# A two-block transformer on one core: high and low weight matmuls in turn in eight of the stages

## The reference

```python
# first block
z = rms_norm(x) @ w_in                       # q, k, v, u, g
h = x + mixed @ w_out                        # mixed: attention and gated MLP
f = rms_norm(h)
h = h + (silu(f @ ffn_w1) * (f @ ffn_w3)) @ ffn_w2      # 2048 -> 5632 -> 2048
h = h + (p @ pl_w_up) * sigmoid(h @ pl_w_gate)
# second block, with 16 tokens put in front
proj = rms_norm(h) @ w_in_2                  # pool, conv and gate inputs
y_b = (gb_in * causal_depthwise_conv(gc_in * v_in, conv_w)) @ conv_out_w
h = h + (g_a * y_a + g_b * y_b) @ w_o
h = h + (silu(gate) * up) @ w_down           # gate, up = rms_norm(h) @ w_gate_up
out = rms_norm(h)
```

## Time and profile before

| | |
|---|---|
| median of 3 runs | 2713.7 us |
| profiled execution, whole | 2712.95 us |
| its span, first to last instruction | 2711.1 us |
| mean granted TensorE clock | 0.996 |
| TensorE busy with matmuls | 2683.8 us, 99% |
| VectorE busy | 1674.7 us, 62% |
| ScalarE busy | 1269.5 us, 47% |
| read from memory | 499.41 MB, 185 GB/s |

### The profile page before, as it was taken

How to read it: one execution, slowest core, us unless ns; L and a number is a source line. 1 busy time by engine, 2 the same in 40 slices (tenths; PEclk the granted TensorE clock), 3 DMA queues, 4 the chain that set the end, 5 groups by cost and what they waited for, 6 DMA issues and landing times.

```text
span 2711.1 us, 40123 instructions
## 1 busy us (share of the span) xinstructions
PE 2683.8 (99%) x15739; PEld 2380.8 (88%) x15739; DVE 1674.7 (62%) x1605; ACT 1269.5 (47%) x1354; POOL 0.8 (0%) x7
## 2 busy tenths in 40 slices
PE   9998999999999999999999999999999999999998
PEld 8888888888888888888999999888888888888887
DVE  6567766555655566696576656556765655565555
ACT  5455554444444444566443333444554434443445
POOL 0000000000000000000000000000000000000000
PEclk9998999999999999999999999999999999999999
DMA  8553555555555555555546555555555555555553
GB/s 294 188 171 115 178 190 189 190 190 189 186 186 187 188 190 188 179 186 187 185 158 202 178 180 187 186 186 186 188 198 189 186 192 192 190 186 191 181 186 140
DMA packets 253935, 504.02 MB, mean 186 GB/s; under 512 B 8082, under 2 KB 11076, under 8 KB 253668
## 3 DMA queue, kind: packets, MB, share of 16 engines
q1 hardware_dynamic: 251860, 497.60, 55.3%
q10 hardware_dynamic: 1952, 4.73, 0.5%
HBM read 499.41 MB, written 2.88 MB: 185 GB/s over the span
## 4 chain that ended last, share of the span: by engine, by line
PE 95%; DVE 3%; ACT 1%; issue 1%; DMA 0%; SPq 0%; DVEq 0%; ACTq 0%
PE ps L1260 47%; PE ps L1266 24%; PE ps L1279 4%; PE ps L1280 4%; PE ps L1281 4%; PE ps L1298 3%; PE ps L1297 3%; PE ps L1299 3%; DVE lo L777 1%; DMA xtok<-in_x_dram 0%; PE ps L1289 0%; PE ps L1291 0%; PE ps L1290 0%; ACT hi L472 0%; DVE work L785 0%
## 5 line engine op out<-in xcount | busy, mean ns | idle before, releaser
L777 DVE TENSOR_TENSOR lo<-raw,hi 128x1024 fp32r<-128x1024 f32 x940 | 1136.9, 1223 | 821.7 <-ACT hi L472 819.1
L472 ACT ACTIVATE hi<-raw 128x1024 fp32r<-128x1024 f32 x940 | 984.9, 1056 | 999.3 <-PE ps L1266 695.8
L1260 PE MATMUL ps<-A,hi 128*128 128x512 f32 x3648 | 914.0, 392 | 1.5 <-DVE work L785 1.5
L1260 PEld LDWEIGHTS ps<-A,hi 128*128 128x128 f32 x3648 | 656.4, 189 | 119.3 <-DVE work L785 1.7
L1266 PEld LDWEIGHTS ps<-A,lo 128*128 128x128 f32 x3648 | 497.6, 190 | 35.7 <-DVE lo L777 0.2
L1266 PE MATMUL ps<-A,lo 128*128 128x256 f32 x3648 | 508.7, 282 | 0.0
L1260 PE MATMUL ps<-B,hi 128*128 128x512 f32 x1984 | 499.6, 393 | 0.3 <-ACT hi L472 0.3
L1260 PEld LDWEIGHTS ps<-B,hi 128*128 128x128 f32 x1984 | 356.1, 188 | 66.1 <-ACT hi L472 0.5
L1266 PEld LDWEIGHTS ps<-B,lo 128*128 128x128 f32 x1984 | 269.8, 189 | 20.6
L1266 PE MATMUL ps<-B,lo 128*128 128x256 f32 x1984 | 275.6, 281 | 0.0
L1297 PE MATMUL ps<-B,hi 128*128 128x258 f32 (+1 forms) x768 | 218.5, 285 | 1.1 <-issue 1.1
(11 more groups left out here) (228 smaller groups left out, 1348.7 us busy)
## 6 DMA issues: line engine op xcount, KB each, us to landing
raw<-in_w_in_dram SPq DMA_DIRECT2D x136, 1024.0 KB, 5.1
raw<-in_ffn_w_dram SPq DMA_DIRECT2D x132, 1024.0 KB, 5.1
raw<-in_w_gate_up_dram SPq DMA_DIRECT2D x88, 1024.0 KB, 5.0
raw<-in_w_down_dram SPq DMA_DIRECT2D x44, 1024.0 KB, 5.0
raw<-in_w_out_dram SPq DMA_DIRECT2D x16, 1024.0 KB, 5.2
raw<-in_pl_w_gate_dram SPq DMA_DIRECT2D x16, 1024.0 KB, 5.1
raw<-in_conv_out_w_dram SPq DMA_DIRECT2D x16, 1024.0 KB, 5.0
raw<-in_w_o_dram SPq DMA_DIRECT2D x16, 1024.0 KB, 5.1
```

Source lines behind the costliest of these rows:

```text
L472: act.activation(hi[:, slot % RING], raw[:, raw_slot, 2 * (slot % 2):2 * (slot % 2) + 2, :], ACT.Copy).then_inc(hi_ready, 1)
L777: dve.tensor_tensor(lo[:, slot % RING], raw[:, slot // 2 % RAWS, 2 * (slot % 2):2 * (slot % 2) + 2, :], hi[:, slot % RING], ALU.subtract). ...
L1260: pe.matmul(to, high(slot, kk, m), both, start=j == 0 and kk == 0, stop=False)
```

## The change

Eight stages are named in a set: the six of the first FFN, `cout` and `wo`. In these a piece no longer runs eight high matmuls and then eight low ones. It waits for `lo_ready` at its start (and no longer for `hi_ready`), and for each block and bank runs the high matmul and right behind it the low one. The other `halves` stages (`qk`, `out`, `plup`, `plgate`, `pool`, the three up-projections of the second FFN), `wide_halves` and the rest keep their order.

```diff
+IN_TURN = {"f1_up0", "f1_down0", "f1_up1", "f1_down1", "f1_up2", "f1_down2", "cout", "wo"}
...
-                if layout in ("halves", "wide_halves") or (layout == "conv" and seg.kinds[g] == "cb"):
+                if seg.name not in IN_TURN and (layout in ("halves", "wide_halves") or (layout == "conv" and seg.kinds[g] == "cb")):
                     pe.wait_ge(hi_ready, n + 1)
...
                     for m in range(MT):
                         Wh, Wl = high(slot, kk, m), low(slot, kk, m)
-                        if layout == "packed":
+                        if layout == "halves":
+                            pe.matmul(ps[:, b0 + m, :], Wh, X[:, k, 0:2 * T], start=first, stop=False)
+                            last = pe.matmul(ps[:, b0 + m, 0:T], Wl, X[:, k, 0:T], start=False, stop=final)
+                        elif layout == "packed":
```

## The result

| | before | changed |
|---|---|---|
| median of the runs | 2713.4 us (2712.0 to 2714.5, 15 runs) | 2719.4 us (2717.4 to 2721.3, 15 runs) |
| span of the profiled execution | 2711.1 us | 2718.0 us |

The ratio is 1.0022, 95% interval 1.0015 to 1.003: slower by 0.22%, where 0.2% faster was forecast. The time lies inside the range, on the other side of no change.

A forecast was written before the change was run, and what follows sets the result against it. The prediction took TensorE's matmul start distances as the bound: 2624 pairs, each 2.2 ns cheaper, save 5.8 us, taking the span from 2711.1 to 2705.3 us and the median to 2708 us. Its 8-in-10 range was 2689 to 2729 us.

The forecast's parts named there:

- What bounds the kernel, and how many pairs change: TensorE, busy 99% of the span, sets the time by distances between matmul starts; 2624 high-low pairs change, 916 us.
- The moved wait: Waiting for lo_ready at a piece's start costs nothing: VectorE's low-part subtraction has at least 1.75 us in hand.
- The start distance read as duration less 162 ns: On TensorE, a matmul's distance to the next start is its shown duration less 162 ns, good to some 2 ns.
- The sum: In the changed stages a pair costs 347 ns (231 high, 116 low), 2.2 ns less than now: 5.8 us saved.
- my upper bound: Highest price of a pair in turn from the rows, 234 + 120 = 354 ns: 13 us lost.
- What a switch between the kinds does: On TensorE, a high soon after lows is up to 7 ns later, a low behind a high some 4 ns sooner.
- The 20 ns that I could not place: Loss per piece with one round of switches in the old order: 2794 ns against 2774 at 226.8 and 120.
- the third, in its mild form: High behind a low 234 ns, low 120 with late weight load: 354 ns a pair, 2726 us; whole rival's chance 0.23.
- its strong form: Each of eight switch rounds a piece pays 20 ns: 46 us more, 2760 us; chance 0.23 for both forms together.
- The first (340 to 343 ns): A single low doesn't disturb the highs, settled rates hold: 16 to 24 us saved, 2690 to 2697 us; chance 0.18.
- The signs: New profile: highs about 393 ns, lows about 278, unchanged second FFN; under 344 or over 350 ns a pair refutes the forecast.
- The rule weighed: Skill page's TensorE gaps, 216 and 109 ns: with a load under each matmul, 325 ns a pair in both orders.

## Why the prediction was wrong

- **What bounds the kernel, and how many pairs change**: right. Only TensorE's start distances moved, on 2624 pairs.
- **The moved wait**: right. It costs nothing in the eight stages, and the run with all stages in turn shows what it costs where the 1.75 us of the earlier trace rows are missing.
- **The start distance read as duration less 162 ns**: right for means (399 + 281 less 353.3 leaves 163 each), but not within 2 ns for one matmul. The trace of before, from start to start, has 233 ns for the first high at 905.20 where I took 234, and 113 for the first low at 907.04 where I took 116.
- **The sum** is the step that failed: "I take the middle of 340 and 354, 347 ns". Its bounds held, and 346.7 is what the fast stages measured. But it made one price for all pairs out of local readings taken in another order, and there are two prices. That 346.7 agrees with the forecast's 347 is in part luck: I took a middle between two bounds, while the fast rhythm is the sum of the settled rates, 226.8 + 120 = 346.8, which stood in the prediction only as the 2774 ns of a piece. In 2112 of 2624 pairs the price is 353.3, 0.7 ns below my upper bound; mis-sized by 6.3 ns there, 13.3 us.
- **What a switch between the kinds does** gave the wrong model, in which a matmul's distance depends on the one before it. The 20 ns that I could not place can be placed by the start distances of before, from 905.20: the eight highs take 233, 236, 228, 233, 231, 226, 227, 227 ns, 27 more than eight settled ones, and the lows 113, 119 and then 120 each, 8 less than eight settled ones. So five highs pass until the rate is settled. In turn it never gets there: in the slow rhythm highs take 233, 236 and 241, the last more than any high of that piece, and three pairs cost 1060 ns where the settled rates give 1040, the same 20 once more. How late a high is depends on several matmuls before it.
- **The rivals**: the third, in its mild form (354 ns, 2726 us), is what the first FFN did as a number; its strong form, 7 more rounds at 20 ns, did not happen. The first (340 to 343 ns) happened nowhere: in turn no high takes less than 230 ns. The convolution's output and the last projection did what the forecast said, 346.7. That different stages could go different ways was among none of them.
- **The signs**: they worked. Highs at 399 ns and 353.3 ns a pair in the first FFN said that the forecast was wrong, and that it was the slower rival; the second FFN kept its times.
- **The rule weighed**, the gaps of the Trainium skill, TensorE: Matmul & The Clock Gate, section "Back-to-back issue gap" (which gives them for a matmul apart from its weight load), would have made the order indifferent. The runs disagree, with 2773 to 2827 ns for a piece of the same matmuls.
- **The range** held the time, because it took the upper bound in.

What stays open is what in TensorE holds the rhythm, and by what rule a start or a break selects one. The runs show that the extra time of a piece fits steps of about 6.7 ns, that the rhythm goes with the stream's own past, and that a break or a stall can change it. They don't show which unit it is, and none of the models here would have told in advance which stages go fast.

## What to carry to other kernels

Where TensorE never waits and a profile still shows it above its settled rates, print the distances from start to start of single matmuls: a repeating pattern with a few ns too many can be a state of the stream rather than a price of the instructions, and the same matmuls can differ by 2% by it (2773 to 2827 ns a piece here). Don't work out a new order from the first matmul behind a switch in the old one; measure each stage, and look at the stages apart, since a whole can hide two opposite changes. A rhythm in which a stream is stuck could be changed here by one short foreign instruction, but also by a stall of 1.7 us, and the way in isn't safe against changes ahead of it, so it has to be checked in the trace of the final kernel.

## What the runs showed of the hardware

- High and low matmuls in turn have two lasting rhythms on TensorE at the same clock (1.00): 1060 ns for three pairs and 693 ns for two. Each held through stages of up to 64 pieces and across their boundaries.
- One loop body in one execution ran in both, turn by turn (16 pieces each), so neither its text nor its addresses alone decide.
- A 128x128 transpose between pairs costs some 0.12 us: the next two distances from high to high are 0.39 and 0.43 us instead of 0.35. Where it brought the fast rhythm to 256 pieces, these took 256 x 54 ns = 13.8 us less.
- Behind eight lows the highs take 233, 236, 228, 233 and 231 ns before they settle at 226 to 227.
- A low matmul of 256 columns starts 112 to 120 ns ahead of the next matmul; a high takes 230 to 241 ns in turn, and 227 only behind several other highs.
